# Sums of squares for normalizing delta-rule keys and queries and attention queries: two rounded products (high part and rest) in place of one F32 product

## What is computed

```python
def l2_norm(x):
    xf = x.astype(jnp.float32)
    return xf * lax.rsqrt(jnp.sum(xf * xf, axis=-1, keepdims=True) + EPS)
...
    q = l2_norm(q.reshape(B, T, A_HEADS, A_DK)) * (A_DK ** -0.5)
    k = l2_norm(k.reshape(B, T, A_HEADS, A_DK))
...
    q = rms_norm(q.reshape(B, T, B_Q_HEADS, B_HD), q_gain) * (B_HD ** -0.5)
```

## Time and profile before

| what | value |
| --- | --- |
| time before, median of 3 runs | 2700.43 us (2695.47 to 2704.51) |
| the profiled execution's own time | 2704.8 us |
| its span, first to last instruction | 2702.8 us |
| PE busy | 2649.8 us, 98% of the span |
| DVE busy | 1546.5 us, 57% |
| ACT busy | 1001.2 us, 37% |
| POOL busy | 359.6 us, 13% |
| mean granted TensorE clock | 0.990 of full speed |

### The profile page before, as it was taken

How to read it: one execution, slowest core, us unless ns; L and a number is a source line. 1 busy time by engine, 2 the same in 40 slices (tenths; PEclk the granted TensorE clock), 3 DMA queues, 4 the chain that set the end, 5 groups by cost and what they waited for, 6 DMA issues and landing times.

```text
span 2702.8 us, 37579 instructions
## 1 busy us (share of the span) xinstructions
PE 2649.8 (98%) x14653; PEld 2119.0 (78%) x14653; DVE 1546.5 (57%) x2261; ACT 1001.2 (37%) x1414; POOL 359.6 (13%) x330
## 2 busy tenths in 40 slices
PE   7999999999999999999999999999999999999999
PEld 5787878787777768888888888888888764888887
DVE  6666756676666664444635444654444776645445
ACT  4544446356655542222342222332222313422223
POOL 1110101021000021111121111121112121211110
PEclk8999999999999999999979999999999999999999
DMA  3222222132222213222212322222322452222231
GB/s 115 81 82 75 78 64 94 39 103 71 78 70 78 78 48 109 93 93 93 93 47 94 105 97 93 93 94 96 106 93 94 119 159 56 94 94 93 98 104 62
DMA packets 171509, 238.23 MB, mean 88 GB/s; under 512 B 6513, under 2 KB 149371, under 8 KB 171411
## 3 DMA queue, kind: packets, MB, share of 16 engines
q1 hardware_dynamic: 163523, 217.23, 24.4%
q0 software_dynamic: 6080, 19.43, 2.6%
q10 hardware_dynamic: 1808, 0.21, 0.1%
HBM read 232.36 MB, written 4.40 MB: 88 GB/s over the span
## 4 chain that ended last, share of the span: by engine, by line
PE 88%; DVE 6%; ACT 2%; DMA 2%; issue 1%; POOL 1%; DVEq 0%; ACTq 0%; POOLq 0%
PE ps L382 20%; PE ps L384 20%; PE ps L383 20%; PE ps L795 5%; PE ps L797 4%; PE ps L796 4%; DVE w_lo L359 1%; DVE probs L1722 1%; PE ps L368 1%; PE ps L369 1%; PE ps L370 1%; PE ps L1574 1%; DMA glu_scratch<-glu 1%; PE ps L1585 1%; PE ps L2072 1%
## 5 line engine op out<-in xcount | busy, mean ns | idle before, releaser
L354 ACT ACTIVATE w_hi<-w_raw 128x2048 fp32r<-128x2048 f32 x203 | 388.5, 1914 | 889.4 <-PE ps L384 882.6
L382 PE MATMUL ps<-h_hi,w_hi 128*128 128x512 f32 x1456 | 567.7, 390 | 1.2 <-DVE w_lo L359 1.2
L384 PE MATMUL ps<-h_hi,w_lo 128*128 128x512 f32 x1456 | 566.6, 389 | 0.0
L383 PE MATMUL ps<-h_lo,w_hi 128*128 128x512 f32 x1456 | 566.4, 389 | 0.0
L359 DVE TENSOR_TENSOR w_lo<-w_raw,w_hi 128x2048 fp32r<-128x2048 f32 x203 | 464.8, 2290 | 130.8 <-ACT w_hi L354 130.8
L427 DVE SCALAR_TENSOR_TENSOR xT<-ps,xT 128x512 f32<-128x512 f32 x488 | 325.6, 688 | 137.1 <-PE ps L384 136.2
L382 PE MATMUL ps<-a_hi,w_hi 128*128 128x512 f32 x992 | 386.3, 389 | 5.3 <-issue 3.5
L384 PE MATMUL ps<-a_hi,w_lo 128*128 128x512 f32 x992 | 385.9, 389 | 0.0
L383 PE MATMUL ps<-a_lo,w_hi 128*128 128x512 f32 x992 | 385.9, 389 | 0.0
L1807 POOL TENSOR_TENSOR f_gate<-f_gate,n_rstd 128x512 f32<-128x512 f32 x88 | 176.9, 2012 | 1123.8 <-ACT f_gate L1801 1123.8
L382 PEld LDWEIGHTS ps<-h_hi,w_hi 128*128 128x128 f32 x1456 | 273.3, 188 | 60.6 <-issue 2.5
(11 more groups left out here) (346 smaller groups left out, 2928.4 us busy)
## 6 DMA issues: line engine op xcount, KB each, us to landing
w_raw<-in_ffn_w_in_dram SPq DMA_DIRECT2D x88, 1024.0 KB, 5.0
w_raw<-in_ffn_w_out_dram SPq DMA_DIRECT2D x44, 1024.0 KB, 4.8
w_raw<-in_a_w_in_dram SPq DMA_DIRECT2D x24, 1024.0 KB, 5.3
w_raw<-in_b_w_in_dram SPq DMA_DIRECT2D x16, 1024.0 KB, 5.4
w_raw<-in_conv_w_pw_dram SPq DMA_DIRECT2D x12, 1024.0 KB, 5.6
shifted<-glu_scratch POOLq DMA_DIRECT2D x32, 264.0 KB, 4.6
w_raw<-in_a_w_out_dram SPq DMA_DIRECT2D x8, 1024.0 KB, 4.8
w_raw<-in_b_w_out_dram SPq DMA_DIRECT2D x8, 1024.0 KB, 4.8
```

Source lines behind the costliest of these rows:

```text
L354: nc.scalar.activation(w_hi[:, t % 2], w_raw[:, t % 2], ACT.Copy).then_inc(hi_done, 1)
L382: nc.tensor.matmul(dst, wh, xh, start=(k == 0), stop=False)
L383: nc.tensor.matmul(dst, wh, xl, start=False, stop=False)
L384: m = nc.tensor.matmul(dst, wl, xh, start=False, stop=last)
```

## The change

Each square is now held in two parts of the F32R type. ACT writes the square once more, rounded (`hi`), DVE subtracts it from the exact square (`lo`), and PE multiplies the ones, also in F32R, with both parts into one bank. The parts lie over buffers that are free at that time: in the delta rule over lower_T and qk_T (high parts) and over decay and expg (rests), which the pass before has read for the last time; in attention the high part over q_cur's half that `scores(3)` reads last, and the rest over q_sq itself. PE's two products of a sum both wait for the rest. In the attention steps `pe_q_squares` moves from behind `turn(2)` to behind `turn(3)`. ACT makes ones_r once, before the first pass.

```diff
@@ buffers
+            ones_r = sb("ones_r", [P, P], F32R, into=s)
+            sq_parts = sb("sq_parts", [P, 8, T], F32R, into=s)
+        sq_hi = {c: sq_parts[:, 4 + (c + 2) % 4] for c in range(4)}
+        sq_lo = {c: sq_parts[:, (c + 2) % 4] for c in range(4)}
-            head_ones = sb("head_ones", [P, P], into=s)
+            head_ones = sb("head_ones", [P, P], F32R, into=s)
+            q_hi = sb("q_hi", [P, 2, 2, T], F32R, into=s)
+            q_lo = sb("q_lo", [P, 2, T], F32R, into=s)
@@ pe_a
             for c in (2, 3, 0, 1):
-                a_act.wait(pe, f"sq{c}", i)
-                a_pe.done(f"ss{c}", mm(ps[:, (6, 7, 4, 5)[c]], ones[:], square[:, c], start=True, stop=True))
+                a_dve.wait(pe, f"lo{c}", i)
+                mm(ps[:, (6, 7, 4, 5)[c]], ones_r[:], sq_hi[c], start=True, stop=False)
+                a_pe.done(f"ss{c}", mm(ps[:, (6, 7, 4, 5)[c]], ones_r[:], sq_lo[c], start=False, stop=True))
@@ act_a_first
             act_decays(act)
+            gates_act.wait(act, "kdec")
+            nc.scalar.activation(ones_r[:], ones[:], ACT.Copy).then_inc(ones_ready, 1)
             round_tile(act, 4)
@@ act_a
                 a_act.done(f"sq{c}", fn(square[:, c], qkv[:, c], ACT.Square))
+                a_pe.before(act, "o31", i)
+                a_act.done(f"hi{c}", fn(sq_hi[c], qkv[:, c], ACT.Square))
             if last:
                 take_z(1)
             rounded(2 if last else 1)
@@ dve_a
             split(2 if last else 1)
+            for c in (2, 3, 0, 1):
+                a_act.wait(dve, f"hi{c}", i)
+                a_dve.done(f"lo{c}", v.tensor_tensor(sq_lo[c], square[:, c], sq_hi[c].bitcast(F32), ALU.subtract))
@@ act_kv
                 act_q_take(act, c, T_B, None, -1, 1)
+            act_q_hi(act, -1, 1)
             round_tile(act, T_B + 2)
@@ dve_kv, behind the copies kt0 and kt1
+            dve_q_lo(dve, -1, 1)
             split_tile(dve, T_B + 2)
@@ pe_q_squares
             for c in range(2):
-                q_act.wait(pe, f"sq{c}{pp}", j)
-                q_pe.done(f"ss{c}{pp}", nc.tensor.matmul(ps[:, bank + c], head_ones[:], q_sq[:, c], start=True, stop=True))
+                q_dve.wait(pe, f"lo{c}{pp}", j)
+                nc.tensor.matmul(ps[:, bank + c], head_ones[:], q_hi[:, pp, c], start=True, stop=False)
+                q_pe.done(f"ss{c}{pp}", nc.tensor.matmul(ps[:, bank + c], head_ones[:], q_lo[:, c], start=False, stop=True))
@@ pe_b
             turn(2)
-            if not last:
-                pe_q_squares(pe, j, pp)
             fill(3)
             values(2)
             fill(2)
             turn(3)
+            if not last:
+                pe_q_squares(pe, j, pp)
             fill(3)
             values(3)
@@ new
+        def act_q_hi(act, j, pp):
+            b_pe.wait(act, f"S3{pp}", j)
+            for c in range(2):
+                q_act.wait(act, f"sq{c}{pp}", j)
+                q_act.done(f"hi{c}{pp}", nc.scalar.activation(q_hi[:, pp, c], q_sq[:, c], ACT.Copy))
+        def dve_q_lo(dve, j, pp):
+            for c in range(2):
+                q_act.wait(dve, f"hi{c}{pp}", j)
+                q_dve.done(f"lo{c}{pp}", nc.vector.tensor_tensor(q_lo[:, c], q_sq[:, c], q_hi[:, pp, c].bitcast(F32), ALU.subtract))
@@ act_b
                 act_q_take(act, 1, t, j, j, pp)
+                act_q_hi(act, j, pp)
             copy(2)
@@ dve_b
             norms(3)
+            if not last:
+                dve_q_lo(dve, j, pp)
             copy(3)
```

More of the change, by code:

```diff
@@ L235, in build @@
         inv_T, neg_wT, k_bg = g_wide, decay, expg
+        with ExitStack() as s:
+            sb("below_ones", [P, 6 * TC * A_HEADS], into=s)
+            ones_r = sb("ones_r", [P, P], F32R, into=s)
+            sb("below_parts", [P, 5 * TC * A_HEADS - P + 2 * (T + TAPS - 1) + 20 * T], into=s)
+            sq_parts = sb("sq_parts", [P, 8, T], F32R, into=s)
+        sq_hi = {c: sq_parts[:, 4 + (c + 2) % 4] for c in range(4)}
+        sq_lo = {c: sq_parts[:, (c + 2) % 4] for c in range(4)}
         binv_T, binv = b_wide[:, 0, 0:8 * BK], b_wide[:, 0, 8 * BK:16 * BK]
@@ L260, in build @@
             probs_T = sb("probs_T", [P, 2, 2, 4, P], into=s)
+        with ExitStack() as s:
+            sb("below_q", [P, NORM_COLS + 4 * T + 2 * T + T + TC * B_HD + P + 2 * 4 * 2 * P + 9 * 8], into=s)
+            q_hi = sb("q_hi", [P, 2, 2, T], F32R, into=s)
+            q_lo = sb("q_lo", [P, 2, T], F32R, into=s)
         with ExitStack() as s:
@@ L624, in build @@
                      + [f"os{a}" for a in heads])
-        a_act = Marks(sem("a_act"), [f"sq{c}" for c in (2, 3, 0, 1)] + [f"ln{c}" for c in (2, 3, 0, 1)]
+        a_act = Marks(sem("a_act"), [x for c in (2, 3, 0, 1) for x in (f"sq{c}", f"hi{c}")] + [f"ln{c}" for c in (2, 3, 0, 1)]
                       + [f"rs{c}" for c in (2, 3, 0, 1)]
@@ L631, in build @@
                       + [f"ors{a}" for a in heads])
-        a_dve = Marks(sem("a_dve"), [f"nrm{c}" for c in (2, 3, 0, 1)]
+        a_dve = Marks(sem("a_dve"), [f"{x}{c}" for x in ("lo", "nrm") for c in (2, 3, 0, 1)]
                       + [f"{x}{a}" for a in heads for x in ("db", "lt")] + ["u0", "u1", "T0", "qk0", "qd0"]
@@ L1390, in build @@
         q_pe = Marks(sem("q_pe"), [f"{x}{pp}" for pp in range(2) for x in ("ss0", "ss1")])
-        q_act = Marks(sem("q_act"), [f"{x}{pp}" for pp in range(2) for x in ("sq0", "sq1", "ln0", "ln1", "rq0", "rq1")])
-        q_dve = Marks(sem("q_dve"), [f"{x}{pp}" for pp in range(2) for x in ("nq0", "nq1")])
+        q_act = Marks(sem("q_act"), [f"{x}{pp}" for pp in range(2) for x in ("sq0", "sq1", "hi0", "hi1", "ln0", "ln1", "rq0", "rq1")])
+        q_dve = Marks(sem("q_dve"), [f"{x}{pp}" for pp in range(2) for x in ("lo0", "lo1", "nq0", "nq1")])
         def pe_kv(pe):
@@ L1457, in act_kv @@
             round_tile(act, T_B + 1)
-            q_act.begin(act, 6)
+            q_act.begin(act, 8)
             b_act.begin(act, 2)
@@ L1478, in dve_kv @@
             v = nc.vector
-            kv_dve.done("zeros", v.memset(head_ones[:], 0.0))
+            kv_dve.done("zeros", v.memset(head_ones[:].bitcast(F32), 0.0))
             kv_dve.wait(dve, "zeros")
-            kv_dve.done("block0", v.memset(head_ones[0:B_HD, 0:B_HD], 1.0))
-            kv_dve.done("block1", v.memset(head_ones[B_HD:P, B_HD:P], 1.0))
+            kv_dve.done("block0", v.memset(head_ones[0:B_HD, 0:B_HD].bitcast(F32), 1.0))
+            kv_dve.done("block1", v.memset(head_ones[B_HD:P, B_HD:P].bitcast(F32), 1.0))
             split_tile(dve, T_KV + 1)
@@ L1513, in dve_kv @@
                     ps[:, 6:8].rearrange("p k t -> p (k t)").rearrange("p (n d) -> p n d", d=B_HD)))
-            q_dve.begin(dve, 2)
+            q_dve.begin(dve, 4)
             b_dve.begin(dve)
+            dve_q_lo(dve, -1, 1)
             split_tile(dve, T_B + 2)
@@ L2438, in build @@
         wab_round, wab_ready = sem("wab_round"), sem("wab_ready")
+        ones_ready = sem("ones_ready")
         def dve_setup(dve):
```

## The result

After the change the kernel takes 2713.84 us (median of 6 runs, 2712.01 to 2716.42), and 2703.03 us before it (median of 6 runs, 2695.47 to 2704.52). The ratio is 1.0042, with a 95% interval of 1.0029 to 1.0054: slower by 0.3 to 0.5%. The profiled execution took 2716.42 us with a span of 2714.7, which is 11.9 us more than the span before.

A forecast was written before the change was run, and what follows sets the result against it. PE, busy 98% of the span, was taken as the bound. Delta rule, key/value part and steps summed to +6.4 us, the clock to +6.2: +12.6 on the profiled 2704.8, or a median of 2713.0 us; range 2703 to 2720.

The forecast's parts named there:

- The saving on PE: All 32 sums: two F32R products take 0.45 us instead of 0.86, saving 0.41 us a sum, 13.1 us in all.
- Rival (d): PE's sums: F32R products on ones and parts cost as much as F32 ones; total +18, 2718 us; chance 0.03.
- The waits: PE before the sums of passes 0 to 3 and the key/value part: waits of 6.8, 2.5, 2.5, 3.4 and 2.3 us.
- Rival (b): PE's sums: subtractions are ready in time, no waits arise, the 13.1 us come in full, 2687.3 us; chance 0.05.
- The delta rule without the clock: Passes 0 to 3: PE is through with the sums later by 5.6, 1.3, 1.3 and 2.2 us.
- The clock: PE behind the new waits: half rate costs +2.0 us in pass 0 and +1.4 for each of three others, +6.2.
- Rival (a): Only the long wait lowers the clock, or later waits take delay back: at most +8.4 us, 2708.8 us; chance 0.21.
- The key/value part: Shared key/value part before attention: PE waits 2.3 us for the first rest and is through with two sums +1.7 us later.
- The steps: Seven attention steps: no wait of PE, each saves 0.8 us, 5.7 us in all.
- Rival (c): Attention steps: the 0.3 us cover breaks, `values(2)` waits 0.5 us in each, +3.5 us, 2716.5 us; chance 0.09.
- The sum: Whole kernel: +6.4 us from waits less savings and +6.2 from the clock, +12.6 us in total.

The follow-up runs named there:

- rests first: The changed kernel with the four subtractions of each delta-rule pass ahead of DVE's split instead of behind it; 2703.07 us, ratio 0.9994.
- kv first too: As rests first, with the two subtractions of the key/value part also moved ahead of the copies there; 2697.72 us, ratio 0.9979.
- extra copies: The changed kernel with two more ACT copies ahead of `copy(2)` in each of the seven attention steps; 2719.92 us in one run.
- warm in waits: The changed kernel with 7, 2, 2 and 3 unread F32 products on PE ahead of the sums in passes 0 to 3; 2714.06 us, ratio 1.0038.
- attention only: The changed kernel with the delta rule put back as before, keeping the change in the key/value part and attention steps; 2699.62 us, ratio 0.9984.
- delta only: The changed kernel with attention put back as before, keeping only the delta-rule part of the change; 2714.39 us, ratio 1.0037.
- all covered: As kv first too, with pass 0's subtractions placed between the taps of DVE's convolution; 2695.35 us, ratio 0.9976.

## Why the prediction was right

The forecast was 2713.0 us and slower at 0.74; measured were 2713.84 and a ratio whose interval lies above no change. The mechanism was right. That the time fits to 0.8 us is partly luck: the change was forecast as +12.6 us and is +10.8 between the medians and +11.4 by the ratio, and it was put on a median of three runs, 2700.43, where the six runs have 2703.03. By its steps:

**The saving on PE.** 0.41 us a sum: four sums gain 1.57 us in passes without a wait, and a step gains 5.72 / 7 = 0.82 us. Rival (d) is out. Its +18 was also too low for what it supposed: with sums of 0.86 us PE and not the rests would have set the pace, for about 5 us more.

**The waits.** Forecast 6.8, 2.5, 2.5, 3.4 and 2.3 us, measured 6.72, 2.44, 2.44, 3.33 and 2.27. The profile counts from the modelled end of the product before; counted as in the forecast, from the time at which PE could have started, the wait of pass 0 is 96.12 - 89.24 = 6.88 us (89.24 is 0.17 later than in the kernel before). The forecast is 0.1 short there since PE followed the start of the rests by 0.82 us and not 0.74. Moving the subtractions alone removed those of passes 1 to 3 (rests first) and that of the key/value part (kv first too), so the place in DVE's queue was the cause. Rival (b), that they don't arise, is what these kernels were made into, and they go to the side it named, if not by its 13.1 us.

**The delta rule without the clock.** Forecast 5.6, 1.3, 1.3 and 2.2 us; with PE kept busy through the waits 5.75, 1.40, 1.40 and 2.28, the same 0.1 more.

**The clock.** The terms were right in size: 2.0 for pass 0 and 1.4 for each other fall, against 1.8, 1.3, 1.4 and 1.3. I had counted the wait of 3.4 us and two of the other three; it was the two of 2.44 us, and not the one of 2.27 in the key/value part. The count was a choice between +2.0 and +7.6 and no reading, and it came out by luck: with the same code in the key/value part the clock fell in three of the other kernels, and pass 0 cost less in two others (below). The rule of the Trainium skill (TensorE: Matmul & The Clock Gate, Part 1: The HAM clock gate), full rate when busy and half when idle and nothing between, agrees with the windows, which show 0.50 and 1.00; taken to say that every wait costs the clock it would have given one fall more than the trace of the kernel after shows. Rival (a), in which only the long wait lowers the clock, fell with the windows of passes 1 to 3; its other half, that later waits take the delay back, shows as no more than 0.1 us from keys 3 to the norm.

**The key/value part.** Forecast +1.7 us; from norm to step 0 the kernel after loses 18.44 - 16.68 = 1.8.

**The steps.** Forecast -5.7; measured -5.72. In the six other kernels that have these steps as they are, the seven gave 5.0 to 5.4 us, since their first step waits longer for DVE's division. Rival (c) did not come: no wait of PE at `values(2)`, and extra copies shows how little cover there was.

**The sum.** To step 7 the terms give 5.6 + 1.3 + 1.3 + 2.2 + 1.7 - 5.7 + 6.2 = +12.6, and the trace +12.72. The span ends at +11.9: behind step 7 the kernel is the same, and it has 3.4 us less at the low clock there (below), which is enough for the 0.8 us. The ratio of the runs gives 0.0042 x 2703 = +11.4 us.

What I missed was in the expectations of the experiments: that a wait left in place would cost the same in each kernel. The one of 2.3 us in the key/value part cost 1.8 us in the kernel after and in extra copies, and 3.3 to 3.4 in three others. And a PE that comes earlier waits anew, at L892 and in the first step, which took back 1 to 3 us of what the better kernels should have gained.

## What to carry to other kernels

When a product is split into parts, the work that makes the parts must be ready before the engine that it relieves gets there: here 13 us saved in instructions became 11 us lost, and with nothing but the subtractions moved ahead of work that is not yet needed, 6 to 11 us gained. Read on each helping engine what stands ahead of the new instruction in its queue, add it up to a time, and compare it with the time at which PE arrives; that was exact here to 0.1 us for the five new waits. Read on from there too: behind a wait that is removed stands the next one. Price a new wait of a busy PE at its length plus what the clock takes after it, and keep that second part as a range. Not tried here: PE's product with the high part needs no rest, so the high products could have gone ahead while PE waited for DVE.

## What the runs showed of the hardware

**The clock behind equal waits.** PE's wait in the key/value part was 2.26 or 2.27 us in five kernels. The granted clock stayed at 1.00 in the kernel after and in extra copies, and fell to 0.50 in rests first, warm in waits and attention only (3.4 us at the low level each). Before the wait PE was busy with the same products in all five. The length of a wait alone doesn't tell whether the clock falls.

**The price behind equal waits.** The wait in pass 0 was 6.72 us in the kernel after, delta only and extra copies, with 6.8 us at the low level in each; the clock came back 4.7, 3.5 and 3.0 us after PE resumed, and the sums of the pass cost 7.5, 7.0 and 6.8 us. In the kernels "rests first" and "kv first too" the wait was 4.53 and 4.52 us, with 3.4 and 6.8 us at the low level and a cost of 4.7 and 5.6 us. (A cost is the offset at keys 0 less the offset at which PE arrived at the sums.)

**Each execution has its own low stretches.** By the records of the profiled executions, without the stretch that begins behind PE's last product, the clock was at 0.50 for 54.6 us before, 68.3 after, and between 27.3 (all covered) and 71.7 us (delta only) in the others. The four falls in the passes are 17 us of it in the kernel after (6.8 + 3 x 3.4), and its total is 13.7 above the kernel before. The rest differs in code that the change doesn't touch: the stretch at 953 to 960 us of the kernel before was 3.4 instead of 6.8 us, that at 1376 to 1394 was 13.7 instead of 17.1, and one of 3.4 at 2302 us of the kernel after was not there before. The kernel before ran in 2693.8 us with a mean clock of 0.994 and in some 2705 with 0.989. A gain or loss of a few us by the clock drowns in this; the offset of one instruction between two traces doesn't, and it is where the terms above were read.
